# Seven block products in place of eight in the feed-forward in-projections of a two-block transformer kernel

## What is computed

```python
D_FF = 2816
def swiglu(x, w_in, w_out):
    a, b = jnp.split(x @ w_in, 2, axis=-1)
    return (jax.nn.silu(a) * b) @ w_out

h = h + 0.5 * rms_norm_2(swiglu(rms_norm_2(h, g_ffn1_pre), w_ffn1_in, w_ffn1_out), g_ffn1_post)
```

## Time and profile before

| | |
|---|---|
| median of 3 runs | 2242.71 us (2233.61 to 2247.63) |
| profiled execution | 2243.71 us, span 2241.9 us |
| PE busy | 94% of the span |
| DVE, ACT, POOL busy | 44%, 32%, 28% |
| chain that ended last | PE 89%, DVE 8%, ACT 2% |
| L704, the matmuls of all weight chunks, in that chain | 68% |

### The profile page before, as it was taken

One profiled execution on the slowest core, in us unless ns is written; L12 is line 12 of the kernel. 1 busy time (PEld: TensorE's weight loads), 2 busy tenths in 40 slices (PEclk: granted clock), 3 DMA queues, 4 the chain that ended last, 5 costly groups with the idle time before them and its releaser, 6 DMA issues.

```text
span 2241.9 us, 28339 instructions
## 1 busy us (share of the span) xinstructions
PE 2103.8 (94%) x11650; PEld 1754.6 (78%) x11650; DVE 993.0 (44%) x1483; ACT 725.9 (32%) x919; POOL 624.9 (28%) x152
## 2 busy tenths in 40 slices
PE   4999989999979999989999997999999979999997
PEld 3697777888757666589999996878788768888885
DVE  7374587656366666442222326232333252223224
ACT  6531345222245555332121123343232232221222
POOL 1331323344200000024433441221244314444440
PEclk6998999999979999989999997999999969999997
DMA  8122114554127999612222221211122212222220
GB/s 257 39 76 93 57 57 132 188 178 160 38 94 277 343 346 341 211 57 77 93 94 94 83 85 38 76 38 57 57 94 94 94 38 94 94 94 94 94 94 38
DMA packets 175177, 261.03 MB, mean 116 GB/s; under 512 B 12169, under 2 KB 140858, under 8 KB 175086
## 3 DMA queue, kind: packets, MB, share of 16 engines
q1 hardware_dynamic: 173550, 257.65, 34.5%
q10 hardware_dynamic: 1536, 2.10, 0.3%
HBM read 257.62 MB, written 2.11 MB: 116 GB/s over the span
## 4 chain that ended last, share of the span: by engine, by line
PE 89%; DVE 8%; ACT 2%; issue 1%; DMA 1%; DVEq 0%; SPq 0%; ACTq 0%
PE PS L704 68%; PE PS L1236 7%; PE PS L1258 4%; DVE Hf L2101 1%; PE PS L1390 1%; DVE macc L2167 1%; DVE Hf L2082 1%; PE PS L1202 1%; PE PS L764 1%; PE PS L1278 1%; DVE R L2113 1%; PE PS L1342 1%; PE PS L779 1%; PE PS L906 0%; PE PS L1160 0%
## 5 line engine op out<-in xcount | busy, mean ns | idle before, releaser
L663 POOL TENSOR_TENSOR w_lo<-w_raw,w_hi 128x2048 fp32r<-128x2048 f32 x133 | 620.3, 4664 | 1527.9 <-ACT w_hi L1509 1527.9
L704 PE MATMUL PS<-HH,w_hi 128*128 128x512 f32 (+1 forms) x1936 | 602.9, 349 | 31.8 <-DVE HL L2075 27.3
L704 PE MATMUL PS<-HL,w_hi 128*128 128x512 f32 (+1 forms) x1936 | 600.6, 348 | 0.0
L704 PE MATMUL PS<-HH,w_lo 128*128 128x512 f32 (+1 forms) x1936 | 597.6, 346 | 0.0
L1509 ACT ACTIVATE w_hi<-w_raw 128x2048 fp32r<-128x2048 f32 x133 | 254.8, 1915 | 713.5 <-DMA w_raw<-in_w_ffn_in 296.0
L704 PEld LDWEIGHTS PS<-HH,w_hi 128*128 128x128 f32 x1936 | 339.8, 191 | 84.4 <-issue 35.9
L704 PEld LDWEIGHTS PS<-HH,w_lo 128*128 128x128 f32 x1936 | 339.4, 191 | 45.8
L704 PEld LDWEIGHTS PS<-HL,w_hi 128*128 128x128 f32 x1936 | 339.3, 191 | 44.8
L2798 DVE TENSOR_TENSOR actf<-PS,sg 128x528 f32<-128x528 f32 (+1 forms) x44 | 30.8, 699 | 428.8 <-PE PS L704 428.8
L2809 DVE TENSOR_TENSOR yacc<-yacc,PS 128x528 f32<-128x528 f32 (+1 forms) x176 | 122.3, 695 | 106.2 <-PE PS L704 106.2
L2691 DVE TENSOR_TENSOR m_lo<-m_raw,m_hi 128x2048 fp32r<-128x2048 f32 x56 | 128.3, 2292 | 77.5 <-ACT m_hi L1842 76.8
(11 more groups left out here) (429 smaller groups left out, 2583.9 us busy)
## 6 DMA issues: line engine op xcount, KB each, us to landing
w_raw<-in_w_in SPq DMA_DIRECT2D x49, 1024.0 KB, 5.0
w_raw<-in_w_ffn_in SPq DMA_DIRECT2D x44, 1024.0 KB, 4.9
m_raw<-in_w_exp_gate SPq DMA_DIRECT2D x56, 512.0 KB, 4.2
m_raw<-in_w_exp_up SPq DMA_DIRECT2D x56, 512.0 KB, 5.3
m_raw<-in_w_exp_down SPq DMA_DIRECT2D x56, 512.0 KB, 4.8
w_raw<-in_w_ffn_out SPq DMA_DIRECT2D x22, 1024.0 KB, 4.8
mod_late<-in_w_mod SPq DMA_DIRECT2D x16, 1024.0 KB, 5.3
mod_early<-in_w_mod SPq DMA_DIRECT2D x8, 1024.0 KB, 11.8
```

The costliest lines, as they stand in the source:

```text
L663: pool.tensor_tensor(w_lo[:, s, :], w_raw[:, s, :], w_hi[:, s, :].bitcast(F32), ALU.subtract).then_inc(split, 1)
L704: ins = mm(o, l, r, **k)
```

## The change

Each gate or up chunk, all 22 of each layer, is computed by a Strassen scheme. The chunk's weight is cut into four blocks (features 0 to 511 or 512 to 1023 of the first 128 hidden columns are `a11` and `a12`, of the last 128 `a21` and `a22`), and `Hf` into four blocks: features 0 to 511 or 512 to 1023, tokens in two halves of H = T/2 columns. Seven products of 128 x H from 4 feature tiles each (`seven_products`) take the place of eight.

- DVE forms block sums of the weights ahead of their split: four additions of 128 x 512 per gate or up chunk (`weight_sums`), one of them in place, three into the new tile `wx_raw`. ACT makes `wx_hi` and POOL `wx_lo` of those three (128 x 1536). `w_hi` now waits for the sum in place, and POOL's split for all four.
- DVE and POOL form block sums of `Hf` and their `lo` parts at the start of a layer (`h_blocks` on either engine), ACT their `hi` parts.
- A gate or up chunk takes four PSUM slots (before two), read by DVE in seven operations (`block_sums`), ACT copying the first product to `fp`. ACT's Silu now works on `sg` in SBUF.
- DVE multiplies `actf` by `sg` in two halves, after tiles 1 and 2 of the down chunk before (`gated`), ACT makes `ah` (`product_hi`), and DVE subtracts `al` in two halves ahead of the next gate chunk's sums (`gated_lo`).
- `mod_sum` is three additions in a tree (1024, 512 and 256 columns) in place of one reduction.

The down chunks stay as they are.

```diff
             def split_chunk(c, s, more=0):
                 pool.wait_ge(hi_done, c + 1 + more * RING)
                 pool.tensor_tensor(w_lo[:, s, :], w_raw[:, s, :], w_hi[:, s, :].bitcast(F32), ALU.subtract).then_inc(split, 1)
+            def split_seven(c, s, more=0):
+                pool.wait_ge(wx_ready, seven_made(c) + 1 + more * 2)
+                split_chunk(c, s, more)
+                pool.wait_ge(hix_done, seven_made(c) + 1 + more * 2)
+                pool.tensor_tensor(wx_lo[s][:, :, :, :], wx_raw[s][:, :, :, :], wx_hi[s][:, :, :, :].bitcast(F32),
+                                   ALU.subtract).then_inc(splitx, 1)
+            def h_blocks(n, T):
+                H, base = T // 2, HH_AT_FF[n]
+                pool.wait_ge(hh_ready, base + KT)
+                pool.tensor_tensor(HL[:, 4:8, 0:H], ...).then_inc(hp_ready, 1)
+                pool.tensor_tensor(HXr[:, 1, :, 0:H], ...).then_inc(t3_ready, 1)
...
+                pool.tensor_tensor(HLx[:, 1, :, 0:H], ...).then_inc(hp_ready, 1)
+                pool.tensor_tensor(HL[:, 4:8, H:T], ...).then_inc(hp_ready, 1)
...
+            def seven_products(T, h_from=None):
...
+                for n in range(7):
+                    if n == 3:
+                        pe.wait_ge(splitx, xcount["n"] + 1 + xcount["more"])
...
+                    if n % 2 == 0:
+                        s = W.claim()
...
+                    for k in range(4):
+                        for x, (l, r) in enumerate(((0, 0), (0, 1), (1, 0))):
+                            ins = product(PS[:, s, n % 2, 0:H], left[l][n][:, k, :], right[r][n][:, k, :],
+                                          start=k == 0 and x == 0, stop=k == 3 and x == 2)
...
+            def weight_sums(c):
...
+                dve.wait_ge(w_in_sem[s], 16 * (c // RING + 1) + more * 16)
+                a11, a12, a21, a22 = weight_blocks(w_raw[:, s, :])
+                x = wx_raw[s]
+                tt(x[:, 1], a11, a21, ALU.subtract)
+                tt(a21, a21, a22, ALU.add).then_inc(wn_ready, 1)
+                dve.wait_ge(wn_ready, n + more * 2)
+                L(tt(x[:, 0], a21, a11, ALU.subtract))
+                tt(x[:, 2], a12, x[:, 0], ALU.subtract).then_inc(wx_ready, 1)
...
             for m in range(KT):
                 s = W.arrive()
                 W.release(stt(R[:, m, META:TALL], ps(s), modc[:, 40 + m:41 + m], R[:, m, META:TALL], ALU.mult, ALU.add))
+                if m in (4, 6):
+                    weight_sums(FF_AT[0] + m // 2 - 2)
...
+                def block_sums(dst):
+                    s0 = W.arrive()
...
+                    tt(dst[:, 0, 0:H], fp[:, 0:H], PS[:, s0, 1, 0:H], ALU.add)
+                    W.skip(1)
+                    s1 = W.arrive()
+                    u_ = L.mark(tt(fu[:, 0:H], fp[:, 0:H], PS[:, s1, 1, 0:H], ALU.add))
+                    L.wait(u_)
+                    w_ = L.mark(tt(dst[:, 0, H:T], fu[:, 0:H], PS[:, s1, 0, 0:H], ALU.add))
+                    dve.sem_inc(free[s0], 1)
...
-                def down():
+                def down(n=None, c=None):
                     for m in range(KT):
                         s = W.arrive()
                         y = sv(yacc[:, m, 0:T], T)
                         W.release(tt(y, y, ps(s, T), ALU.add))
+                        if m in (1, 2) and n is not None:
+                            gated(n, m - 1)
+                        if m == 4 and c is not None:
+                            weight_sums(c)
...
+                def unit(n, c, par):
+                    gated_lo(n - 1, 1 - par)
+                    gates()
+                    if c is not None:
+                        weight_sums(c)
+                    block_sums(actf)
+                    down(n, None if c is None else c + 1)
...
-                v_.tensor_reduce(macc[:, d % 2, :].unsqueeze(2), mod_early[n][:, :, :].rearrange("p k n -> p n k"), AX, ALU.add).then_inc(
-                    macc_ready, 1)
+                raw = mod_early[n]
+                L(tt(raw[:, 0:4, :], raw[:, 0:4, :], raw[:, 4:8, :], ALU.add))
+                L(tt(raw[:, 0:2, :], raw[:, 0:2, :], raw[:, 2:4, :], ALU.add))
+                tt(macc[:, d % 2, :], raw[:, 0, :], raw[:, 1, :], ALU.add).then_inc(macc_ready, 1)
```

More of the change, by code:

```diff
@@ L472, in build, with seven, seven_made, weight_blocks @@
         block = ctx.enter_context(nc.Block())
+        FF_AT = (BEFORE_MOE, BEFORE_MOE + n_ff + n_p2 + n_m2 + n_wo)
+        HH_AT_FF = (2 * KT, 4 * KT + 12)
+        def seven(c):
+            for b in FF_AT:
+                if 0 <= c - b < n_ff - 1:
+                    return c - b < 2 or (c - b - 2) % 3 < 2
+            return False
+        def seven_made(c):
+            return sum(seven(x) for x in range(c))
+        def weight_blocks(w):
+            w = w.rearrange("p (k n) -> p k n", k=KT)
+            return w[:, 0:4, 0:P], w[:, 4:8, 0:P], w[:, 0:4, P:2 * P], w[:, 4:8, P:2 * P]
         def mod_dve(n):
@@ L1434, in _ @@
             norm(SEQ)
[L1435 to L1436 removed]
+            swiglu(1, FF_UNITS, SEQ)
             norm(SEQ)
@@ L1911, in _, with swiglu, silu, product_hi @@
             W.skip(KT)
-            def swiglu(units, T, last=False):
-                def gates(waits):
-                    b = W.g
-                    next_hi()
[L1917 to L1921, removed]
-                    next_hi()
[L1923 to L1929, removed]
+            def swiglu(units, T):
+                base = n_["ff"]
+                def silu(n):
+                    act.wait_ge(gate_sum, base + n + 1)
+                    af(sg[:, :, 0:T], sg[:, :, 0:T], ACT.Silu).then_inc(gate_silu, 1)
+                def product_hi(n, par):
+                    act.wait_ge(actf_ready, base + n + 1)
+                    af(ah[:, par, :, 0:T], actf[:, :, 0:T], ACT.Copy).then_inc(ah_ready, 1)
+                def first_product():
+                    s = W.arrive()
+                    af(fp[:, 0:T // 2], PS[:, s, 0, 0:T // 2], ACT.Copy).then_inc(fp_ready, 1)
+                    W.skip(4)
+                def unit(n, par):
+                    first_product()
+                    next_hi()
+                    silu(n)
+                    first_product()
+                    next_hi()
+                    product_hi(n, par)
+                act.wait_ge(hp_ready, 3 * (base // units) + 3)
+                unit(0, 0)
+                c0, g0 = hi["c"], W.g
+                pairs = (units - 1) // 2 - 1
@@ L1930, in swiglu @@
                 with act.Fori(0, pairs) as i:
-                    W.g, W.more = g0, i * 6
                     hi["c"], hi["rounds"] = c0, i * 2
-                    for _ in range(2):
-                        gates(True)
+                    W.g, W.more = g0, i * 8
+                    for par in (1, 0):
+                        unit(i * 2 + (2 - par), par)
                         next_hi()
                         W.skip(KT)
-                W.g, W.more = g0 + 24 * pairs, 0
                 hi["c"], hi["rounds"] = c0 + 6 * pairs, 0
-                for n in range(2 * pairs, units):
-                    if n + 1 < units:
-                        gates(True)
+                W.g, W.more = g0 + 32 * pairs, 0
@@ L1942, in swiglu @@
+                for n in range(2 * pairs + 1, units):
+                    unit(n, n % 2)
                     next_hi()
                     W.skip(KT)
-            norm(TALL, every)
+                next_hi()
+                W.skip(KT)
+                n_["ff"] += units
+            norm(TALL, every, split="blocks")
             swiglu(FF_UNITS, TALL)
@@ L2043, in _ @@
             norm(SEQ, y_real, split=False)
-            norm(SEQ, real, tiles=False)
-            swiglu(FF_UNITS, SEQ, last=True)
+            norm(SEQ, real, tiles=False, split="blocks")
+            swiglu(FF_UNITS, SEQ)
             norm(SEQ, y_real, split=False)
@@ L2114, in apply_rms @@
                     dve.wait_ge(r_ready, n_["r"])
+                elif split == "blocks":
+                    h_blocks(T)
                 elif split:
```

240 lines of the change are left out of this document (187 added, 53 removed).

## The result

The changed kernel takes 2262.43 us (median of 5 runs, 2259.55 to 2270.74), the kernel before 2245.02 beside it: ratio 1.0092 (formed from all runs; the two medians alone give 1.0078), 95% interval 1.0063 to 1.012. It is 0.9% slower, at the edge of what I had called no change. The forecast was 2277 in a range of 2224 to 2308. The profiled span is 2260.4 us where it was 2241.9: +18.5 us, against +32.9 forecast.

A forecast was written before the change was run, and what follows sets the result against it. TensorE's matmuls were taken to bound both feed-forwards. Opening -2.1, entrances +17.7 and +7.1, layers -3.1 and +13.3 sum to +32.9 us on 2243.71, about 2277 us; 80% range 2224 to 2308, own range 2262 to 2295.

The forecast's parts named there:

- Matmuls: Feed-forward units: fewer or shorter matmuls save 59 us together, leaving TensorE 32.3 us a unit in FF1, 31.0 in FF2.
- The port and its turns: DVE operations with two SBUF inputs wait for POOL's whole instruction, up to 4.6 us; whoever has waited longer goes next.
- DVE keeps the port: Rival: in the units `al` half 1 follows half 0 without waiting, TensorE is the limit; about 2236 us, chance 0.16.
- POOL keeps it: Rival: POOL holds the port between neighbouring instructions, making the unit loop 38.3 us; 2360 us, chance 0.10.
- The port costs nothing on the path: Rival: TensorE stays the limit in the units; -46 us in all, 2198 us, chance 0.16.
- The units: Nine units a layer at 33.8 us in FF1 and 33.7 in FF2: -13.0 and +2.3 us.
- The last step: End of an FF2 unit: `al` half 1, then three block sums, free slot 0 33.7 us after TensorE starts the up chunk.
- Start and end of a layer: Waits less shorter chunks: starts +9.2 us in FF1 and +10.0 in FF2, ends +0.7 and +1.0.
- the rival of the clock: Rival: waits in the units lower TensorE's clock, 1.5 us a unit, 27 us more; 2304 us, chance 0.08.
- Entrances: Ahead of each feed-forward's first product, chunk preparation and additions of squares are delayed: +17.7 us into FF1, +7.1 into FF2.
- The opening: Additions replace reductions, but the last addition waits for POOL's first split to 45.2 us: -2.1 us; without that wait -6.5.
- the one with 0.21: Whole kernel: the case that the time stays within about 1% of the kernel before, chance 0.21.

The follow-up runs named there:

- Run 2: The changed kernel with `al` as one DVE instruction of both halves in place of two: 2239.49 us, ratio 0.9988 to the kernel before.
- run 1: The kernel before with the opening's six reductions done as three additions each: 2238.14 us, ratio 0.9984 to the kernel before.
- run 3: The changed kernel with POOL's `wx_lo` subtraction cut from 1536 columns to 128, leaving out part of the computation: 2230.73 us, ratio 0.9943 to the kernel before.
- run 7: The kernel before with opening sums as two additions, then one reduction over the last two rows: 2235.57 us, ratio 0.9973.
- run 8: The changed kernel with `al` joined, entrances reordered, memsets moved and the opening ending in a reduction: 2207.44 us, ratio 0.9851 to the kernel before.
- run 4: The changed kernel with the preparation of each feed-forward's first two chunks reordered, with one semaphore: 2244.57 us, ratio 1.0016 to the kernel before.
- run 6: The changed kernel with the `yacc` memsets moved behind the block sums of gate 0: 2260.04 us, ratio 1.0085 to the kernel before.
- run 5: The changed kernel with the edits of run 2 and run 4 together: 2217.52 us, ratio 0.990 to the kernel before.

## Why the prediction held, and what was off

**Matmuls.** I had TensorE's own time as 32.3 and 31.0 us a unit. Run 2 shows it bare: 32.15 and 30.97.

**The port and its turns** held in every place that was forecast: `al` waits twice, `actf` once, chunk 1's sums, the additions of squares, the last step of the opening. Runs 1, 2, 3 and 7 each change one side of it (who asks, how often, for how long, with which operation), and the wait follows. The rivals *DVE keeps the port* and *POOL keeps it* fall with the pair of 8.02 us between two longer instructions of POOL. *The port costs nothing on the path* gave 2198 us; the changed kernel is 64 us above that, and run 8 comes to 2207.

**The units** were mis-sized, and this is the largest term: 33.8 and 33.7 us forecast, 33.24 and 33.13 measured, nine of each, 5.0 and 5.1 us. In FF2 the chain agrees with my steps to 0.4 us up to `al`: split of gate n+1 at S+8.6, `actf` half 0 at 13.6, `al` half 0 asking at 24.1 with S = 2097.44. The last step was too dear. The pair of `al` ended at S+32.1 and not 32.4. And I had put three block sums of 0.43 us behind it. They follow each other in 0.33 and 0.44 us, and DVE gives the slot back while the third is still running (it begins at 2097.26, TensorE starts at 2097.44), so 0.9 us and not 1.3.

**Start and end of a layer**: +12.3 and +11.8 against +9.9 and +11.0. In FF1 the step that fell short is the clock: I had given the first two products to half speed, 5 us. The windows of FF1's first 35 us, of the three stretches at the lower level in it, and of one unit each of FF2 and FF1 show it lower for longer:

```profile
992.42:1027.42 35.00, 26.42 (x155) 25.47 (x156) 28.73 (x32) 13.44 (x12) 22.13 (x7) 0.73 0.18 60
992.42:997.70 5.28, 4.88 (x20) 4.58 (x21) 5.17 (x3) 1.90 (x2) 5.28 (x2) 0.50 0.60 199
1001.10:1007.90 6.80, 4.68 (x22) 4.40 (x21) 6.80 (x3) 1.48 (x2) 6.03 (x2) 0.50 0.00 0
1014.70:1021.60 6.90, 5.22 (x24) 5.25 (x25) 3.25 (x9) 1.08 (x1) 4.74 (x2) 0.51 0.46 149
2097.44:2130.38 32.94, 31.25 (x216) 28.91 (x217) 27.45 (x35) 11.32 (x9) 21.65 (x6) 1.00 0.29 96
1205.38:1238.55 33.17, 32.36 (x264) 32.18 (x265) 27.38 (x35) 11.48 (x9) 21.68 (x6) 1.00 0.28 95
```

TensorE works 14.8 us at the lower level, which costs half of that, 7.4 us (an estimate); the kernel before has 5.4 us of it there and loses 2.7. So the clock took 4.7 us more than I had. The pauses were 5.0 us shorter than forecast: 4.6 us in the first chunk (7 forecast), 4.0 for the slot (5.3) and none ahead of up 1 (1.3). Near the end the wait for `al` is 2.9 us (2.2), and 3.0 us of work at the lower level behind it cost another 1.5. Together that is +1.9 of the +2.4. The two large terms had thus missed by 5 us each way and nearly cancelled, which is luck. In FF2, with 0.73 in its first 35 us as well, they cancel in the same way. Run 2 has 0.86 where this trace has 0.73, and its first `al` comes 1.3 us sooner after the first product, so a part of the loss is scatter as well.

In FF1's units the clock stayed at 1.00. In FF2's it fell to the lower level three times for 3.4 us (at 1932.9, 2031.9 and 2165.0), but TensorE has slack there and the units keep to 32.9 to 33.3 us. So the rival of the clock, 1.5 us in each unit, did not come about; run 4 has two such drops at FF2's end, and there they cost.

**Entrances**: +16.8 and +6.0 against +17.7 and +7.1. Run 4 shows their cause, since order alone gives back 14.8 and 5.2 us. One link was missing from my account: the small operation on `gain`, below.

**The opening**: -2.4 against -2.1, with the 4.64 us that I had taken from the port. I had the reduction at 44.20 inside POOL's split. It only begins there (POOL ends at 45.18, the reduction at 47.80), which is enough for the reading, since it takes no longer than 3.60 us; run 7 then shows a whole reduction beside POOL.

**The mixer's -4.9** was in no step, and it is not the change's. TensorE's program is the same there. Windows of the kernel before, then of the changed one, from the same point of the program:

```profile
1497.89:1500.89 3.00, 1.76 (x16) 1.56 (x16) 1.71 (x3) 2.04 (x7) 0.89 (x1) 1.00 0.00 0
1500.89:1503.89 3.00, 3.00 (x23) 2.24 (x20) 1.65 (x4) 0.06 (x1) 0.00 (x0) 0.76 0.00 0
1503.89:1506.89 3.00, 3.00 (x8) 1.43 (x7) 0.99 (x1) 2.14 (x6) 0.00 (x0) 0.50 0.00 0
```

```profile
1506.23:1509.23 3.00, 1.77 (x17) 1.57 (x17) 1.70 (x3) 2.04 (x7) 0.88 (x1) 1.00 0.00 0
1509.23:1512.23 3.00, 3.00 (x26) 2.14 (x23) 1.65 (x4) 0.07 (x1) 0.00 (x0) 1.00 0.02 5
1512.23:1515.23 3.00, 3.00 (x15) 1.68 (x14) 0.99 (x1) 2.12 (x6) 0.00 (x0) 1.00 0.00 0
```

After the same pause of 1.24 us the granted clock falls to 0.50, the lower of its two levels (1.2 GHz), in the one and stays full in the other. The stretch from the fourth `ql` to DVE's first `pc` takes 86.10 us or 81.28. Of the other traces, run 7, which is the kernel before but for the opening, has 81.35; run 6, which is nearly the changed kernel, has 86.16; run 1 has 86.16, run 8 84.55, and runs 2 to 5 have 81.3. So it falls out one way or the other with kernels that are alike there, and the change is not the cause. The Trainium skill, TensorE: Matmul & The Clock Gate, section Part 1: The HAM clock gate, says that the monitor runs free of the program, so that the same kernel is slowed for different lengths of time at its start. These ten traces show a like spread behind a pause in the middle.

With the terms together: -10.1 in the units, +3.2 at starts and ends, -2.0 at entrances, -0.5 before them and -4.9 in the mixer take the forecast of +32.9 to the measured +18.5. A third of the miss was thus scatter between two single executions, and the rest size. The time lies at the very edge of my own range (2262 to 2295), and the case to which I gave 0.60, over 1% slower, did not come; the one with 0.21 did. That chance leaned on the unit's last step: with the measured 33.24 and 33.13 in place of 33.8 and 33.7 the sum would have been 2267. A slip that changes nothing: by its own steps *DVE keeps the port* comes to -4 and not -3 in FF2, and to 2234 us.

## What to carry to other kernels

Count how often an engine has to ask for a port that it shares, not only how long it holds it. Where two engines take turns and both have work waiting, each DVE instruction with two SBUF inputs costs one of POOL's, so two halves cost two and one joined instruction costs one: here one line was worth 1.0%. And when a change makes another engine prepare operands, look first at what stands in that engine's queue at the entrance of the stage: order alone was worth 20 us, as much as the change had saved in the units of both layers.

## What was not expected of the hardware

A tensor-scalar operation of 128x8 with one SBUF input took 4.50 us beside POOL's split (969.52, L3075), where it takes 0.17 with POOL idle. I had counted only operations with two SBUF inputs. The Trainium skill, SBUF — State Buffer, section Who interferes with whom, names tensor-scalar operations among those that can contend with GpSimd for the shared port pair, under conditions on their operands. The trace agrees, even at eight columns. A scalar-tensor-tensor operation of 128x8, with two SBUF inputs, took 2.40 us in run 7 and 0.17 in run 1, where POOL was idle. At such sizes the wait is all of the cost, so a tiny operation waits for POOL's instruction like a big one.
